# Key turns and scores one w_in slot sooner, the first two value products in the last two slots, and the first heads' products ahead of the wait for the chunk state's copy

## The chip, the cores and the metric

One core of a Trainium2 chip runs the whole step in one launch. The metric is the device time of one execution in microseconds, as the median of several runs. The engines are TensorE (PE; its weight loads are shown apart as PEld), VectorE (DVE), ScalarE (ACT), GpSimd (POOL) and SyncE (SP, which only issues DMAs here). Each engine works off its own list of instructions in order, and waits on semaphores that the others count up.

## What is computed

Two layers of a hybrid decoder, for a prompt of 256 tokens and 8 sampled sequences of 8 tokens, which makes T = 320 columns everywhere. Each layer is a half FFN, a mixer and another half FFN. The mixer, cut from the reference:

```python
z = h @ p['w_in']
gq, gk, gv, gg, glr, sq, sk, sv, cu = jnp.split(z, offs, axis=-1)
# gated linear attention over gq, gk, gv, in chunks with a carried state
o_gla, s_new = gla_chunked(q, k, v, log_a, s0)
# stick-breaking attention over paged keys and values of 2048 past tokens
#   z = q.k/sqrt(d) + bias;  w = exp(log_sigmoid(z) + sum of log(1-beta) over later keys)
o_sb = stick_breaking(q_sb, k_all, v_all, p['sb_bias'], q_pos, k_pos)
# causal depthwise conv (31 taps) over cu, LayerNorm, swish
mix = jnp.concatenate([o_gla, o_sb, y], axis=-1)
return mix @ p['w_out'], k_new, v_new, s_new, buf_new
```

The part that this change touches is the stick-breaking attention of the 64 sampled tokens over their cached keys, from the last pages to the first, since each weight needs the sum over all later keys.

## The kernel before

**Units.** A weight matrix goes through in tiles of 128 output columns, called units. Each is loaded by SP into one of eight slots of `raw`, split by ACT (`hi`, line 1119) and DVE (`lo`, line 1470) into a rounded part and a rest, and multiplied by PE with three matmuls for each of eight k tiles (lines 571 to 573), 24 in all. `w_in` has 23 units. The loops over m = 4 to 22 on PE, ACT and DVE are each one program step for one unit; "slot m" below is that step. Each engine has its own loop over m, and the order in it is written out by hand.

**What rides along in the slots.** The cached keys come in 16 half page groups h = 0 to 15, for four batches each. For h there is, in this order: PE turns the keys (`turn_keys`, line 772, eight transposes for two batches, twice), ACT copies them from the bank to `kT` (`copy_keys`, line 1274), PE makes the scores (`scores`, line 787), and for each pair of h, it = 0 to 7, ACT takes the scores out of bank 4 (`place_scores`, lines 1283 and 1284) and makes the softplus (`softplus`, lines 1289 and 1291), DVE sums it up backwards (`log_weights`, lines 1678, 1681 and 1683), ACT takes the exponential (`weights`, line 1296), PE turns the weights (`turn_weights`, line 864), ACT copies them (`place_weights`, line 1301) and PE multiplies them with the pages of values (`values`, line 882). `TURNS` says which h is turned in which slot; `scores(h - 1)` is made at the start of the slot that turns h, ahead of the unit. In slots with two h (10 and 12 before) the second turn and a second score product stand between k tiles of the unit. SP and POOL load the keys of h when h - 2 has been turned (`SLOT_OF`), and the pages of `values(it)` when the room is free.

**What each slot has besides.** `turn_state` at the end of slot 6 and ACT's `place_state` behind it; ACT's `place_queries` in slot 7, which writes the queries to `qb` (line 1237), from which `scores` reads, and which stands behind the first `copy_keys` of the slot; two sigmoids in slot 8; the decays and levels of the gated linear attention in slots 12 to 20 (`decays`, lines 1253 and 1255; `level_prompt` and `level_sample` on PE; `place_prompt`, `place_sample`, `scale` and `decay` on DVE); copies of the conv state in slot 12 (lines 1354 and 1355); the conv taps (line 1619), shared out over the slots by two tables, where taps count by four instructions; and `scaled_in` (lines 1667 and 1672), DVE's read of a unit's bank.

**Behind slot 22.** PE makes the scores of the prompt (`pz_products`, lines 992 and 993), all but the first of which wait for DVE's `scaled_in(22)`. Then come the state products (line 1008), `values(1)`, the wait for ACT's copy of the first state (`s1`, line 1382), `gla_outputs` for heads 0 and 1 (line 943), the wait for DVE's second state (`s2`, line 1805), `turn_weights(3)` (line 864) and so on. Key 0 is turned before the mixer in both layers, key 1 in layer 1 alone (`KEYS_EARLY`).

Of the kernel before, what the change touches and what calls it, by code (L numbers as in the profile page):

```python
# [153 lines left out]
def zin_done(at, m):  # L154

    if m < 13:
        return at("zin_dve", m + 1)
    return at("zin_act", m - 12) if m < 19 else at("zin_dve", m - 5)


def slots():

    slot = []
    for l in range(L):
# [11 lines left out]
BEFORE = [max((v for v in range(u) if SLOT[v] == SLOT[u]), default=None) for u in range(len(SLOT))]  # L176
TAPS_EARLY = {13: 1, 14: 1, 15: 1, 16: 1, 17: 1, 18: 1, 19: 1}
TAPS_LATE = {9: 2, 10: 2, 11: 2, 12: 1, 14: 2, 16: 2, 18: 2, 19: 1, 20: 3, 21: 2, 22: 2}
TURNS = {7: (0,), 8: (1,), 9: (2,), 10: (3, 4), 11: (5,), 12: (6, 7), 13: (8,), 14: (9,), 15: (10,), 16: (11,), 17: (12,), 18: (13,),
         19: (14,), 20: (15,), 21: (16,), 22: (17,)}  # L180
KEYS_EARLY = ((0,), (0, 1))
SLOT_OF = {h: m for m, hs in TURNS.items() for h in hs}
WEIGHTS_AT = {10: 0, 11: 1, 13: 2, 14: 3, 16: 4, 18: 5, 20: 6, 22: 7}
MEAN_BANK = (3, 5, 0, 1)


# [24 lines left out]
def build(nc, ins, outs):  # L211
# [106 lines left out]
    def in_bank(m):  # L318

        return bank[m if m < 7 else (m + 1) % 2]  # L320
# [28 lines left out]
    with nc.Block() as block:  # L349
# [198 lines left out]
        def _(pe):  # L548
# [66 lines left out]
            def x_mean(M, b_):  # L615
                pe.wait_ge(sm["sx_done"], M + 1)
                pe.matmul(b_[:, 0:T], cst_("mean_d"), sx[:, :], start=True, stop=True).then_inc(sm["x_mean"], 1)
# [54 lines left out]
            def keys_early_copied(l2, h):  # L672
                pe.wait_ge(sm["kt_copied"], 64 * l2 + 4 * h + 4)

            for l in range(L):
# [4 lines left out]
                def at(name, n):  # L680
                    return sm[name], l * per[name] + n
# [193 lines left out]
                def values(it):  # L875

                    pe.wait_ge(*at("wt_placed", it + 1))
                    pe.wait_ge(*at(f"vs_loaded{it % 2}", 128 * (it // 2 + 1)))
                    pe.wait_ge(*at(f"vp_loaded{it % 2}", 128 * (it // 2 + 1)))
                    for j in range(4):  # L880
                        for b in range(G):
                            last = pe.matmul(bank[7][32 * b:32 * b + 32, 0:256], wT[:, it, j, 32 * b:32 * b + 32],  # L882
                                             vpg[l][it % 2][:, b, j, :], start=False, stop=(j == 3 and it % 4 == 3), skip_group_check=True)
                    last.then_inc(sm["v_used"], 1)

                entry(U + U_IN, M1, [in_bank(m) for m in range(4)])
                for m in range(4, NIN):
                    u, out = U + U_IN + m, in_bank(m)[:, 0:T]
                    if m < 7:
                        if m == 4:  # L890
                            keys_early_copied(l, l)
                        unit(u, out, hh, hl)
                        if m == 4:
                            x_mean(M1, bank[7])
                        if m == 6:
                            turn_state()
                        continue
                    h, last_h = TURNS[m][0], TURNS[m][-1]
                    if h < 2 * ITS:
                        turn_keys(h, (0, 1))  # L900
                    if 0 < h <= 2 * ITS:
                        scores(h - 1)
                    if m == 8:
                        new_scores()
                    if 14 <= m < 18:
                        level_sample(m - 14)
                    if m == 22:
                        turn_khat()
                    pe.wait_ge(*zin_done(at, m - 7 if m < 9 else m - 2))
                    if h == last_h:  # L910
                        unit(u, out, hh, hl, part=range(4))
                    else:
                        unit(u, out, hh, hl, part=range(3))
                        turn_keys(h, (2, 3))
                        unit(u, out, hh, hl, part=range(3, 5))
                        turn_keys(last_h, (0, 1))
                        unit(u, out, hh, hl, part=range(5, 6))
                        scores(h)
                        unit(u, out, hh, hl, part=range(6, 7))
                    if last_h < 2 * ITS:  # L920
                        turn_keys(last_h, (2, 3))
                    if m == 9:
                        log_gates()
                    if m == 11:
                        turn_rows()
                        new_weights()
                    if m == 12:
                        turn_conv()
                    if 13 <= m < 21:
                        level_prompt(m - 13)  # L930
                    if 14 <= m < 20:
                        turn_values(m - 14)
                    if m == 22:
                        new_values(0)
                        values(0)
                    if m >= 20:
                        turn_weights(m - 20)
                    unit(u, out, hh, hl, part=range(4, KD) if h == last_h else range(7, KD))

                def gla_outputs(pair):  # L940

                    def mm(h, cols, lhs, rhs, first=False, end=False):
                        return pe.matmul(bank[O_BANK[h % 2]][:, cols], lhs, rhs, start=first, stop=end, skip_group_check=True)  # L943
                    vh = [slice(h * DV, (h + 1) * DV) for h in range(H)]
                    for h in pair:
                        mm(h, slice(0, P), gv[:, 0, vh[h]], att[:, 0, h, :], True)
                        mm(h, slice(P, TP), gv[:, 1, vh[h]], att[:, 1, h, :])
                        mm(h, slice(TP, T), gv[:, 2, vh[h]], att[:, 2, h, 0:TS])
                    for h in pair:
                        r, p_ = head(h)  # L950
                        mm(h, slice(P, TP), s1[r, p_, :], qt[r, 0, p_, P:TP])
                    for b in range(DB):
                        c = slice(TP + DT * b, TP + DT * b + DT)
                        for h in pair:
                            r, p_ = head(h)
                            last = mm(h, c, st[r, b, p_, :], qt[r, 0, p_, c], end=(b == DB - 1))
                            if b == DB - 1:
                                last.then_inc(sm["o_prod"], 1)
# [50 lines left out]
                                         kn[:, ch, h * DK:(h + 1) * DK], gv[:, ch, h * DV:(h + 1) * DV], start=True, stop=True, skip_group_check=True)  # L1009
                last.then_inc(sm["s1_prod"], 1)  # L1010

                values(1)
                pe.wait_ge(*at("s1_ready", 1))
                gla_outputs((0, 1))
                pe.wait_ge(*at("s2_ready", 2))
                turn_weights(3)
# [89 lines left out]
        def _(act):  # L1106
# [97 lines left out]
            for l in range(L):  # L1204
# [88 lines left out]
                def weights(it):  # L1293

                    act.wait_ge(*at("lw_ready", it + 1))
                    A(nsa(z_[:, it, :], z_[:, it, :], ACT.Exp), sm["w_ready"])
# [8 lines left out]
                for m in range(7, NIN):  # L1305
                    what = UNITS_IN[m][0]
                    for h in TURNS[m]:
                        if h < 2 * ITS:
# [3 lines left out]
                        if h >= 2 and h % 2 == 0:  # L1312
                            place_scores(h // 2 - 1)
                        if h == TURNS[m][0]:
                            hi(U + U_IN + m + 2)
# [12 lines left out]
                            A(nsa(tn[:, :, :], tn[:, :, :], ACT.Ln, bias=1.0), sm["zn_l"])  # L1328
                        if h >= 2 and h % 2 == 0:
                            softplus(h // 2 - 1)  # L1330
                    if m in WEIGHTS_AT and m < 22:
                        weights(WEIGHTS_AT[m])
                    if m == 9:
                        act.wait_ge(*at("loga_pre", 1))
# [33 lines left out]
                        place_values(m - 14)  # L1368
                    if m >= 20:
                        place_weights(m - 20)  # L1370
                    if m == 22:
                        weights(7)
                    if what in ("gv", "sv"):
                        act.wait_ge(sm["w_used"], U + U_IN + m + 1)
                        A(nsa(fT[:, 4 + (m + 1) % 2, :], in_bank(m)[:, 0:T], ACT.Copy), sm["zin_act"])
# [85 lines left out]
        def _(dve):  # L1461
# [133 lines left out]
            for l in range(L):  # L1595
# [4 lines left out]
                def at(name, n):  # L1600
                    return sm[name], l * per[name] + n
# [72 lines left out]
                def log_weights(it):  # L1674

                    z, s = z_[:, it, :], s_[it % 2]
                    dve.wait_ge(*at("z_l", it + 1))
                    V(dve.scalar_tensor_tensor(t_[:, :], z, 0.0, t_[:, :], ALU.max, ALU.add))
                    V.settle()
                    later = sn[:, it // 4, 0:1] if it % 4 == 0 else s_[1 - it % 2][:, 0:1]  # L1680
                    V(dve.tensor_tensor_scan(s[:, ::-1], cst_("ones", cols=1).to_broadcast([P, 512]), t_[:, ::-1], later, ALU.mult, ALU.add))
                    V.settle()
                    V(dve.tensor_tensor(z, z, s[:, :], ALU.subtract), sm["lw_ready"])
# [9 lines left out]
                for m in range(7, NIN):  # L1693
# [60 lines left out]
                    if 13 <= m < 19:  # L1754
                        if m > 13:
                            dve.wait_ge(*at("att_done", level_copies(m - 14)))
                        place_prompt(m - 13)
                    for h in TURNS[m]:
                        if h >= 2 and h % 2 == 0:
                            log_weights(h // 2 - 1)  # L1760
                    for k in range(TAPS_LATE.get(m, 0)):
                        conv(taps)
                        taps += 1
# [117 lines left out]
def head(h):  # L1881

    return slice((h % 2) * DK, (h % 2 + 1) * DK), h // 2
# [35 lines left out]
```

## Time and profile before

| | us |
|---|---|
| median of 3 runs | 1443.51 |
| lowest, highest | 1441.48, 1445.41 |
| the profiled execution | 1444.73 |
| its span | 1443.1 |
| PE busy | 1405.8 (97%) |
| DVE busy | 899.5 (62%) |
| ACT busy | 738.4 (51%) |

The profiled execution lies 1.2 us above the median. Its span is 1.6 us shorter than its device time. The mixer's slots of layer 0 lie between 274 and 406 us of the span, those of layer 1 706 us later. In the rows, L is a line of the kernel, and a tile is named as out<-in with its buffer number left out.

### The profile page before, as it was taken

The numbers are of one execution on the slowest core, as the hardware profiler recorded it, in microseconds if no ns is written. First come the engines' busy times: TensorE is split into PE (matmuls) and PEld (weight loads), VectorE is DVE, ScalarE is ACT, GpSimd is POOL, SyncE is SP. The second block draws the span as 40 slices with busy tenths as digits, with TensorE's granted clock in tenths as the row PEclk, the third lists the DMA queues.
The fourth block names the chain that finished last, engine by engine and source line by source line (L and its number), as shares of the span: only waits on it lengthen the run. The fifth ranks groups of instructions, "written<-read, shape, count | busy, mean of one in ns | idle before, by whom it ended". The sixth has DMA issues, their size and how long they took to land.

```text
span 1443.1 us, 26817 instructions
## 1 busy us (share of the span) xinstructions
PE 1405.8 (97%) x10515; PEld 1329.7 (92%) x10515; DVE 899.5 (62%) x1496; ACT 738.4 (51%) x1198; POOL 179.6 (12%) x326
## 2 busy tenths in 40 slices
PE   7999999999999999999999999999999999999997
PEld 6999999988877899999999999999887689999996
DVE  5665633679985766653367655355899747766542
ACT  4544433588855544343364444355886555443431
POOL 0020000323254000000000000021423510000000
PEclk9999999999999999999999999999999999999998
DMA  9565555567798575545545555556867894554441
GB/s 239 147 204 150 145 150 156 163 199 223 212 294 270 149 189 153 146 139 156 156 130 151 146 146 146 146 153 176 249 201 232 270 250 130 150 154 146 147 135 37
DMA packets 391362, 250.23 MB, mean 173 GB/s; under 512 B 14369, under 2 KB 379446, under 8 KB 391236
## 3 DMA queue, kind: packets, MB, share of 16 engines
q1 hardware_dynamic: 375602, 205.86, 50.0%
q0 software_dynamic: 15328, 42.52, 9.5%
q8 instruction: 84, 1.38, 0.4%
q14 instruction: 42, 0.34, 0.1%
q10 hardware_dynamic: 306, 0.13, 0.0%
HBM read 242.91 MB, written 5.53 MB: 172 GB/s over the span
## 4 chain that ended last, share of the span: by engine, by line
PE 89%; DVE 5%; ACT 3%; DMA 2%; issue 1%; SPq 0%; ACTq 0%
PE bank L571 23%; PE bank L572 23%; PE bank L573 23%; PE bank L772 3%; PE bank L882 2%; PE bank L607 2%; PE bank L611 2%; PE bank L608 2%; DVE fT L1619 2%; PE bank L787 2%; PE bank L943 1%; PE bank L737 1%; DVE w_l L1470 1%; DMA raw<-in_ffn_w_up 1%; DMA raw<-in_ffn_w_gate 1%
## 5 line engine op out<-in xcount | busy, mean ns | idle before, releaser
L1470 DVE TENSOR_TENSOR w_l<-raw,w_h 128x1024 fp32r<-128x1024 f32 (+1 forms) x334 | 397.6, 1197 | 301.7 <-ACT w_h L1119 301.7
L571 PE MATMUL bank<-hh,w_h 128*128 128x320 f32 x1648 | 517.5, 314 | 0.0
L573 PE MATMUL bank<-hh,w_l 128*128 128x320 f32 x1648 | 509.2, 309 | 0.0
L572 PE MATMUL bank<-hl,w_h 128*128 128x320 f32 x1648 | 509.1, 309 | 0.0
L1119 ACT ACTIVATE w_h<-raw 128x1024 fp32r<-128x1024 f32 (+1 forms) x334 | 334.6, 1030 | 144.2 <-DMA raw<-in_ffn_w_down 98.8
L571 PEld LDWEIGHTS bank<-hh,w_h 128*128 128x128 f32 x1648 | 309.4, 188 | 11.4 <-issue 8.6
L572 PEld LDWEIGHTS bank<-hl,w_h 128*128 128x128 f32 x1648 | 309.6, 188 | 0.5
L573 PEld LDWEIGHTS bank<-hh,w_l 128*128 128x128 f32 x1648 | 309.4, 188 | 0.0
L573 PE MATMUL bank<-guh,w_l 128*128 128x320 f32 x704 | 217.4, 309 | 0.0
L571 PE MATMUL bank<-guh,w_h 128*128 128x320 f32 x704 | 217.4, 309 | 0.0
L572 PE MATMUL bank<-gul,w_h 128*128 128x320 f32 x704 | 217.4, 309 | 0.0
L571 PEld LDWEIGHTS bank<-guh,w_h 128*128 128x128 f32 x704 | 132.2, 188 | 0.0
L572 PEld LDWEIGHTS bank<-gul,w_h 128*128 128x128 f32 x704 | 132.2, 188 | 0.0
L573 PEld LDWEIGHTS bank<-guh,w_l 128*128 128x128 f32 x704 | 132.2, 188 | 0.0
L1188 ACT ACTIVATE sg<-gr 128x320 f32<-128x320 f32 x88 | 41.5, 472 | 170.5 <-DVE gr L1537 170.4
L1193 ACT ACTIVATE guh<-gt 128x320 fp32r<-128x320 f32 x88 | 41.5, 472 | 131.0 <-DVE gt L1548 131.0
L499 POOL DMA_DIRECT2D st<-in_state_gla x4 | 3.6, 900 | 652.6 <-PE bank L573 652.6
L471 POOL DMA_DIRECT2D kpg<-in_cache_sb_k x112 | 60.6, 541 | 163.2 <-PE bank L772 135.6
L1537 DVE TENSOR_TENSOR gr<-bank,rs 128x320 f32<-128x320 f32 x88 | 43.0, 488 | 60.4 <-PE bank L573 45.3
L1619 DVE SCALAR_TENSOR_TENSOR fT<-ext,par_all,fT 128x256 f32<-128x256 f32 x240 | 76.4, 380 | 2.1
L1274 ACT ACTIVATE kT<-bank 128x512 f32<-128x512 f32 x116 | 62.8, 595 | 22.1 <-PE bank L772 21.7
L772 PE MATMUL bank<-const,kpg 128*128 128x128 f32 x448 | 58.5, 273 | 0.7 <-ACT kT L1274 0.7
(268 smaller groups left out, 1601.7 us busy)
## 6 DMA issues: line engine op xcount, KB each, us to landing
raw<-in_ffn_w_gate SPq DMA_DIRECT2D x88, 512.0 KB, 3.9
raw<-in_ffn_w_up SPq DMA_DIRECT2D x88, 512.0 KB, 3.9
raw<-in_ffn_w_down SPq DMA_DIRECT2D x64, 448.0 KB, 3.7
raw<-in_w_in SPq DMA_DIRECT2D x46, 512.0 KB, 4.1
raw<-in_ffn_w_down SPq DMA_DIRECT2D x32, 512.0 KB, 4.0
kpg<-in_cache_sb_k SPq DMA_DIRECT2D x112, 128.0 KB, 3.1
kpg<-in_cache_sb_k POOLq DMA_DIRECT2D x112, 128.0 KB, 2.6
raw<-in_w_out SPq DMA_DIRECT2D x16, 512.0 KB, 8.1
```

The costliest lines, as they stand in the source:

```text
L471: pool.dma_start(heads(kpg[l][:, h % 2, b, j, :]), page(pool, ids[4 * i + 2 * (h % 2) + j], ins["cache_sb_k"], l)).then_inc(sm[f"kp_loaded ...
L571: pe.matmul(out, w_h[:, slot, k, :], rhs_h[:, k0 + k, :], start=first, stop=False)
L572: pe.matmul(out, w_h[:, slot, k, :], rhs_l[:, k0 + k, :], start=False, stop=False)
L573: last = pe.matmul(out, w_l[:, slot, k, :], rhs_h[:, k0 + k, :], start=False, stop=end)
L772: last = pe.transpose(bank[2 + b % 2][:, p_ * 256 + j * P:p_ * 256 + (j + 1) * P], src[:, b, j, p_ * P:(p_ + 1) * P], cst_("ident"))
L1119: A(nsa(w_h[:, slot, 0:n, :], raw[:, slot, 0:n, :], ACT.Copy), sm["w_hi"])
L1188: A(nsa(sg[:, t, :], gr[:, t, :], ACT.Silu), sm["gate_act"])
L1193: A(nsa(guh[:, 2 * i + t, :], gt[:, t, :], ACT.Copy), sm["gu_hi"])
L1274: A(nsa(kT[l][:, h % 2, b].rearrange("p a c -> p (a c)"), bank[2 + b % 2][:, :], ACT.Copy), sm["kt_copied"])
L1470: V(dve.tensor_tensor(w_l[:, slot, 0:n, :], raw[:, slot, 0:n, :], w_h[:, slot, 0:n, :].bitcast(F32), ALU.subtract), sm["w_lo"])
L1537: V(dve.tensor_tensor(gr[:, t, :], ffn_bank(i, 2 * t)[:, 0:T], rs[:, :], ALU.mult), sm["gate_r"])
L1619: V(dve.scalar_tensor_tensor(out, x, par("conv_w", 2 * k + c), out, ALU.mult, ALU.add), sm["conv_y"] if k == TAPS - 1 and c == n == 1 else ...
```

## The change

The key turns 1 to 15 and the scores 0 to 15 are each made one slot sooner: h = 1 in slot 7, and two of them in slots 10 (4 and 5) and 12 (7 and 8). `weights(it)` moves one slot sooner from it = 2 on. DVE's `log_weights` has a table of its own: it = 0 and 1 stay in slots 9 and 10, the others move one slot sooner. `new_values(0)` and `values(0)` move from slot 22 to slot 21, and `values(1)` from behind the state products into slot 22. The wait for `s1_ready` moves into `gla_outputs`, behind the first six products of the two heads.

```diff
-TURNS = {7: (0,), 8: (1,), 9: (2,), 10: (3, 4), 11: (5,), 12: (6, 7), 13: (8,), 14: (9,), 15: (10,), 16: (11,), 17: (12,), 18: (13,),
-         19: (14,), 20: (15,), 21: (16,), 22: (17,)}
+TURNS = {7: (1,), 8: (2,), 9: (3,), 10: (4, 5), 11: (6,), 12: (7, 8), 13: (9,), 14: (10,), 15: (11,), 16: (12,), 17: (13,), 18: (14,),
+         19: (15,), 20: (16,), 21: (17,), 22: (17,)}
...
-WEIGHTS_AT = {10: 0, 11: 1, 13: 2, 14: 3, 16: 4, 18: 5, 20: 6, 22: 7}
+WEIGHTS_AT = {10: 0, 11: 1, 12: 2, 13: 3, 15: 4, 17: 5, 19: 6, 21: 7}
+LOGS_AT = {9: 0, 10: 1, 11: 2, 12: 3, 14: 4, 16: 5, 18: 6, 20: 7}
...
-                    if m == 22:
+                    if m == 21:
                         new_values(0)
-                        values(0)
+                    if m >= 21:
+                        values(m - 21)
...
                         mm(h, slice(TP, T), gv[:, 2, vh[h]], att[:, 2, h, 0:TS])
+                    pe.wait_ge(*at("s1_ready", 1))
                     for h in pair:
...
-                values(1)
-                pe.wait_ge(*at("s1_ready", 1))
                 gla_outputs((0, 1))
...
-                    if m in WEIGHTS_AT and m < 22:
+                    if m in WEIGHTS_AT:
                         weights(WEIGHTS_AT[m])
...
-                    if m == 22:
-                        weights(7)
...
-                    for h in TURNS[m]:
-                        if h >= 2 and h % 2 == 0:
-                            log_weights(h // 2 - 1)
+                    if m in LOGS_AT:
+                        log_weights(LOGS_AT[m])
```

## Rows read from the trace of the kernel before

**Rows 1.** The page, busy time of each engine over the whole span.
```profile
PE 1405.8 (97%) x10515; PEld 1329.7 (92%) x10515; DVE 899.5 (62%) x1496; ACT 738.4 (51%) x1198; POOL 179.6 (12%) x326
```

**Rows 2.** Waits of PE: who waited for whom: us in total, times, longest.
```profile
PE bank L607 <- ACT hh L1146: 8.9, 5, 2.8
...
PE bank L992 <- DVE fT L1672: 2.7, 2, 1.7
...
PE bank L882 <- DMA vpg1a<-in_cache_sb_v: 0.9, 1, 0.9
PE bank L772 <- ACT kT L1274: 0.7, 2, 0.3
PE bank L752 <- DVE att L1651: 0.6, 2, 0.3
```

**Rows 3.** Windows, DVE: stretch, length, busy (instructions), PE's granted clock, DMA.
```profile
345.10:361.90 16.80, 16.52 (x38) 1.00 0.65 189
378.32:408.52 30.20, 28.52 (x65) 1.00 0.75 226
```

**Rows 4.** Timeline, PE, slots 7 and 8, layer 0: start, length, instruction, tiles.
```profile
282.32 0.39 PE L571 MATMUL bank<-hh,w_h 128*128 128x320 f32 x1
...
285.93 1.04 PE L772 MATMUL bank<-const,kpz 128*128 128x128 f32 x8
```

**Rows 5.** Timeline, ACT, slot 7, layer 0.
```profile
284.27 0.82 ACT L1237 ACTIVATE qb<-qs 64x64 f32<-64x64 f32 x4
```

**Rows 6.** Timeline, ACT, slots 12 and 13, layer 0.
```profile
327.04 1.09 ACT L1274 ACTIVATE kT<-bank 128x512 f32<-128x512 f32 x2 [1.12 <-PE bank L772]
328.01 0.74 ACT L1253 ACTIVATE dd<-dd 128x640 f32<-128x640 f32 x1
...
331.57 1.07 ACT L1274 ACTIVATE kT<-bank 128x512 f32<-128x512 f32 x2
332.52 0.69 ACT L1283 ACTIVATE z__105<-bank,bq 128x512 f32<-128x512 f32 x1
...
336.95 0.62 ACT L1296 ACTIVATE z__105<-z__105 128x512 f32<-128x512 f32 x1
```

**Rows 7.** Timelines, PE and ACT, slot 7, layer 1.
```profile
990.04 0.39 PE L571 MATMUL bank<-hh,w_h 128*128 128x320 f32 x1
...
991.98 0.82 ACT L1237 ACTIVATE qb<-qs 64x64 f32<-64x64 f32 x4
```

**Rows 8.** Timeline, PE, slots 12 and 13, layer 0.
```profile
325.86 0.41 PE L571 MATMUL bank<-hh,w_h 128*128 128x320 f32 x1
...
332.29 1.11 PE L772 MATMUL bank<-const,kpg 128*128 128x128 f32 x8
```

**Rows 9.** Timeline, DVE, the scan of a log, slot 15, layer 0.
```profile
355.68 1.29 DVE L1681 TENSOR_TENSOR_SCAN s<-const,sn,t__106 128x512 f32<-128x512 f32 x1
```

**Rows 10.** Timelines, behind slot 22: PE in layers 0 and 1, DVE in 1.
```profile
411.98 2.62 PE L882 MATMUL bank<-vpg0b,wT 128*32 128x256 f32 x32
...
1117.06 1.93 PE L882 MATMUL bank<-vpg1b,wT 128*32 128x256 f32 x32
...
1122.52 0.66 PE L864 MATMUL bank<-const,z__105 128*128 128x128 f32 x4
...
1119.67 0.60 DVE L1805 SCALAR_TENSOR_TENSOR s<-s,aend,bank 128x128 f32<-128x128 f32 x2
```

**Rows 11.** Windows with the clock: all engines; PE alone at both FFN entries.
```profile
410.02:413.43 3.41, 3.41 (x33) 2.35 (x36) 3.19 (x10) 1.31 (x3) 0.00 (x0) 0.50 0.92 291
...
485.11:491.94 6.83, 5.94 (x22) 5.94 (x23) 6.80 (x16) 4.87 (x11) 0.00 (x0) 0.50 0.17 44
...
486.00:502.85 16.85, 16.85 (x97) 0.82 0.02 5
1193.03:1207.35 14.32, 14.32 (x96) 1.00 0.00 1
```

**Rows 12.** Waits of all engines: DVE's logs for ACT's softplus.
```profile
DVE t__106 L1678 <- ACT t__106 L1291: 12.0, 4, 4.8
```

## The prediction

> **What bounds the kernel now.** I read the page's busy times first, then PE's waits, then the timelines of the three compute engines side by side through the mixer of layer 0, from 282 to 415 us, and of layer 1 the same places. PE is busy for 97% of the span [rows 1], so an edit pays only where it removes a wait of PE, and costs wherever it adds one. PE's waits inside the mixer are few [rows 2]: 2.7 us in both layers together for DVE's last `scaled_in` ahead of `pz_products`, 0.9 us for a load of value pages in layer 1, 0.7 us for ACT's key copies (slot 11) and 0.6 us for DVE's `place_prompt` (slot 14). The matmuls, transposes and scores that move are the same in number, so their time is only moved. All that the change can win is therefore about 5 us, and half of it is one wait.
>
> The wait at `pz_products` has a cause of its own. From the end of slot 18 to the last `scaled_in`, DVE is busy for 28.52 of 30.20 us, and in slots 15 and 16 for 16.52 of 16.80 [rows 3]. DVE is a second engine at its limit there, and the change takes no work from it.
>
> **Slot 7, the first key turn and scores.** Before, slot 7 had nothing but the unit's 24 matmuls between `turn_state` and `scores(0)`; these ran from 282.32 to 285.93 us [rows 4]. They covered what ACT must do meanwhile: place the state, split weight tile 8 and only then copy the queries into `qb`, from 284.27 for 0.82 us [rows 5]. After the change `scores(0)` stands ahead of the unit, and it waits for `qb_ready`. In layer 0, PE starts turn 1 at 282.32; eight transposes take 1.0 us (1.04 with the end of the last) [rows 4], so it would be at the scores at 283.3. ACT now has turn 1's first two key copies in front of the queries, since `copy_keys` is called before `place_queries`: 284.27, plus 1.0 for two copies (1.09 with its end) [rows 6], plus 0.82, is 286.1. **PE waits 2.9 us** with the hand-over. In layer 1 key 1 was turned early, so there are no transposes and no copies: PE is there at 990.04 and the queries are ready at 991.98 + 0.82 = 992.8 [rows 7]. **PE waits 2.8 us.** Behind PE's wait stand the unit of slot 7 and everything after it, and no engine has work ahead that could give the time back, because ACT and DVE are fed by PE's units. Sum: +5.7 us. Bounds: 5.5 to 5.9; I find nothing that hides it.
>
> **Slots 8 to 11.** ACT does the first `place_scores` and `softplus` one slot sooner, in the slot with the two sigmoids. Following its queue against PE's, the copies are ready when PE asks for them, in slot 9 with about 0.1 us to spare. In slot 11 ACT no longer has slot 10's `softplus` just ahead of the copies that PE waits for, so the 0.34 us of that wait goes in each layer: -0.7.
>
> **Slots 12 and 13.** Here the change loads ACT. `scores(7)` is now the second score product of slot 12, so `place_scores(3)` and `softplus(3)` stand in slot 12 behind it, with `weights(2)`, all ahead of `decays(1)`, the two copies for the conv state and `decays(2)`, and all of it ahead of the copy of turn 9 that PE needs for the second half of that turn. In the times of the kernel before: the matmuls behind the slot's second score product start at 325.86 [rows 8]; `place_scores` takes 1.2 (two of 0.69), two copies 1.0, `weights` 0.6 (0.62), `softplus` 1.3 (two activations on a tile of the same size as that of `weights`), decays and conv copies 331.57 - 328.01 = 3.56, the first copy of the next turn 0.54, half of 1.09 [rows 6]. That ends at 334.1. PE was at this turn at 332.29 [rows 8]: **1.8 us of waiting**, and 0.3 more where turn 8 in slot 12 finds ACT late from slot 11. Together 2.1 in each layer, +4.2. Bounds: 0 if ACT's queue is shorter than I add it up, 2.6 if nothing overlaps.
>
> **Slots 14 to 19.** The logs now fall into the even slots, where two late conv taps are; odd slots have neither. Two slots take 16.8 us, of which DVE works 16.5 [rows 3], some 8.3 in each; a log is a scan of 1.3 us [rows 9] and two passes of about half of it, 2.7 together. So DVE needs 8.3 + 2.7 = 11.0 us from the start of `place_sample` in an even slot to that in the next. PE asks for the next one after a slot of 8.4 and the stretch from `level_sample` to `level_prompt`, four k tiles of the unit and half a key turn, 2.8: 11.2. With `place_sample` itself (0.5) DVE is late by up to 0.4. Two such places, +0.8 a layer. Slot 14's own wait for `place_prompt` (0.3) goes, as there are no logs in slot 13. Net +0.5 a layer, +1.0. Bounds: -0.6 (only the gain) to +2.
>
> **Slots 18 to 22.** Slots 20 and 21 lose a turn and a score product (3 us), and `values(0)` and `values(1)` (1.93 us each) stand in 21 and 22. PE reaches `pz_products` no later than now, but DVE still has the same 28.5 us behind slot 18. What it can save is its own idle time there, 1.7 us at most [rows 3], hand-overs included. I take 0.7 a layer, about in the middle: -1.4, bounds -2.7 (the whole of the wait) and 0. The value pages are asked for a slot sooner and used a slot sooner; the load's 0.9 us [rows 2] is gone, or falls under the wait for DVE, so it is worth nothing by itself.
>
> **Behind slot 22.** `values(1)` stood between the state products and `gla_outputs`, 1.93 us in layer 1 [rows 10], and hid ACT's copy of `s1`; now the six products of the first heads stand there, so no wait appears. PE is at the turn behind the wait for `s2_ready` at 1122.5 in layer 1; without `values(1)` it is there at 1120.6, and `s2` is written at 1119.67 + 0.60 = 1120.3 [rows 10]. Cost 0, with 0.3 us to spare; up to 0.5 a layer if DVE slips.
>
> **The clock.** New waits of some 3 us matter twice. PE sat idle for 2.8 us at the entry of the second FFN in both layers (its wait for ACT's `hh` [rows 2] is the row of it). In layer 0 the granted clock then was 0.50 (1.2 GHz) for 6.83 us, in layer 1 it stayed at 1.00 (2.4 GHz) behind an idle time of the same length; the same entry matmuls took 16.85 us in the first and 14.32 in the second [rows 11]. A fall so costs 2.5 us. The Trainium skill (TensorE: Matmul & The Clock Gate, the section on HAM oscillation in real kernels) puts the loss at half of the time at half clock; that is an estimate of 3.4 us for these 6.83, and by it my sum would be 0.9 higher. The measured 2.5 stands. The wait of 1.7 us at `pz_products` in layer 0 was also followed by 3.4 us at 0.50: `values(1)` took 2.62 us instead of 1.93 [rows 10, 11]. Of four new waits of 2 to 3 us I count one fall of 2.5 (bounds 0 and three, 7.5), and leave the one at `pz_products` as it is.
>
> **Sum.** 5.7 - 0.7 + 4.2 + 1.0 - 1.4 + 2.5 = +11.3 us. The profiled execution took 1444.73 us (span 1443.1), which gives 1456.0; it stood 1.2 above the median of 1443.51, so I predict **1454.8 us**.
>
> **The rivals.**
> *Only slot 7 waits.* ACT catches up in slot 12 because its steps overlap more than I add; then 4.2 and most of the clock term go: 1443.5 + 5.7 - 0.7 + 1.0 - 1.4 = 1448 without a fall, 1450.6 with one. For it: ACT is busy only 51% of the span [rows 1]. Against: the steps of [rows 6] follow one another without a gap already. Chance 0.20, a third of it within 0.3%.
> *The tail pays it back.* Slot 7 costs its 5.7, but the pz wait (2.7), the load (0.9) and the key copies (0.7) all go, and `values(1)` runs at full clock (0.7): 1443.5 + 0.7 = 1444. It needs DVE to be through 1.3 us sooner in each layer than now. Chance 0.07.
> *Faster: DVE sets the time of the mixer, not PE.* If the chain of slots 14 to 22 on DVE is the bound from end to end, earlier scores let it start its logs sooner (it sat idle for 4.8 us before one of them [rows 12]), the wait in slot 7 is absorbed, and PE's waits of 2.7, 0.9, 0.7 and 0.6 go with the slow `values(1)` (0.7): 1443.5 - 5.6 = 1438. It decides if PE loses less than 1.3 us in slot 7. Chance 0.06.
> *More falls of the clock:* two more, 1454.8 + 5 = 1460. Chance 0.08.
> The forecast itself has 0.59.
>
> **How the numbers follow.** This kernel's measurement can tell 0.3% from no change, 4.3 us: below 1439.2 is faster, above 1447.8 slower. Slower: 0.59 + 0.08 + two thirds of 0.20 = 0.80. Same: 0.07 + 0.07 = 0.14. Faster: 0.06. The range goes from 1447 (only slot 7, most of the pz wait gone) to 1462 (both ACT waits in full, two or three falls) and leaves out the last two cases of the other sign and a little above.
>
> **What would show it.** Right: in the profile after, PE's line of the scores waits for ACT's `qb` copy, 2 times, 5 to 6 us in all; its line of the turns waits for the `kT` copies for 3 to 5 us in slot 13; the pz wait still stands at 1.5 us or more in sum; the window of DVE behind slot 18 holds 28.5 us of work as before. Wrong: a wait for `qb` under 1 us would break the largest step; no wait in slot 13 the second; a pz wait of zero would say that DVE had more to give than its idle time.

## The result, and the profile after

| | before | after |
|---|---|---|
| median, us | 1443.87 (6 runs, 1441.48 to 1445.41) | 1455.56 (6 runs, 1452.45 to 1458.58) |
| ratio | | 1.0087, 95% interval 1.0074 to 1.0100 |
| profiled execution, us | 1444.73 | 1458.58 |
| its span | 1443.1 | 1456.9 |
| PE busy in it | 1405.8 | 1410.4 |
| span less PE busy | 37.3 | 46.5 |

The changed kernel is 11.7 us slower; the forecast was 11.3 (1454.8 us), inside its range. The profiled execution lies 3.0 above the median, so its span is 13.8 longer than that of before. Two of the runs in the next section, one of g2 (1973.1 us) and one of h1 (1540.7 us), were at mean granted clocks of 0.65 and 0.85 and are left out of the medians and ratios.

The first thing to read is the busy line of the page, beside [rows 1]:

```profile
PE 1410.4 (97%) x10515; PEld 1334.7 (92%) x10515; DVE 900.1 (62%) x1496; ACT 739.2 (51%) x1198; POOL 179.2 (12%) x326
```

No engine has another number of instructions, and DVE and ACT are busy for as long as before (within 0.8 us). PE is busy for 4.6 us more with the same 10515 matmuls, and idle for 9.2 us more (46.5 - 37.3). The 13.8 us are the sum of these two. The idle time is in the waits of PE (us in total, times, longest), to be read against [rows 2]; line numbers on PE and ACT are one higher than before, those on DVE one lower:

```profile
PE bank L608 <- ACT hh L1147: 8.9, 5, 2.8
...
PE bank L788 <- ACT qb L1238: 5.4, 2, 2.8
PE bank L883 <- ACT wT L1302: 4.1, 6, 0.7
PE bank L773 <- ACT kT L1275: 3.7, 2, 1.9
PE bank L967 <- ACT wT L1302: 1.4, 1, 1.4
PE bank L995 <- DVE fT L1671: 1.3, 2, 0.7
PE bank L738 <- DVE att L1657: 1.2, 4, 0.3
...
PE bank L883 <- DMA vpg1a<-in_cache_sb_v: 0.8, 1, 0.8
PE bank L851 <- DVE qt L1748: 0.7, 1, 0.7
```

L788 is new, and so are L967, L738 and L851; L773 had 0.7 us in slot 11 and now has 3.7 in slot 13; the wait at `pz_products` (L995) has halved; the one for `place_prompt` is gone. That for the page `vpg1a` is still there (0.8 us, 0.9 before). The timelines of ACT and PE in slot 7 of layer 0 (start, length, instruction, tiles, wait in brackets) show the largest one, where [rows 4, 5] showed none:

```profile
284.34 1.09 ACT L1275 ACTIVATE kT<-bank 128x512 f32<-128x512 f32 x2
285.29 0.83 ACT L1238 ACTIVATE qb<-qs 64x64 f32<-64x64 f32 x4
...
286.27 1.17 PE L788 MATMUL bank<-kpz,qb 128*32 128x256 f32 x16 [2.76 <-ACT qb L1238]
```

PE is through with its transposes at 283.5 and stands still until the second copy of keys and then the four copies of queries are done. In slot 13, ACT's queue ahead of the copy that PE wants is this, against [rows 6, 8]:

```profile
333.81 1.09 ACT L1275 ACTIVATE kT<-bank 128x512 f32<-128x512 f32 x2
334.93 0.63 ACT L1290 ACTIVATE t__106<-t__106 128x512 f32<-128x512 f32 x1
335.59 0.63 ACT L1292 ACTIVATE t__106<-t__106 128x512 f32<-128x512 f32 x1
336.13 0.62 ACT L1297 ACTIVATE z__105<-z__105 128x512 f32<-128x512 f32 x1
336.65 0.72 ACT L1254 ACTIVATE dd<-dd 128x640 f32<-128x640 f32 x1
...
340.18 1.07 ACT L1275 ACTIVATE kT<-bank 128x512 f32<-128x512 f32 x2
...
340.90 1.29 PE L773 MATMUL bank<-const,kpg 128*128 128x128 f32 x8 [1.87 <-ACT kT L1275]
```

The 4.6 us of PE's busy time are its clock. The windows behind the four long waits (length, then PE, PEld, DVE, ACT and POOL busy, then the granted clock) show 0.50 each time, that is 1.2 GHz; before, no such stretch stood in the slots:

```profile
287.10:290.50 3.40, 3.40 (x19) 3.13 (x13) 1.23 (x1) 0.11 (x1) 0.00 (x0) 0.50 0.02 5
341.70:345.10 3.40, 3.40 (x23) 2.85 (x21) 3.37 (x7) 3.35 (x6) 2.18 (x4) 0.50 0.44 122
1000.50:1003.90 3.40, 3.40 (x19) 2.95 (x12) 1.23 (x1) 1.94 (x3) 0.00 (x0) 0.50 0.00 0
1055.10:1058.50 3.40, 3.40 (x21) 3.18 (x18) 3.37 (x8) 2.57 (x5) 1.93 (x4) 0.50 0.52 154
```

Behind slot 22 is a wait that the prediction did not have, at the head means (L967):

```profile
423.84 0.63 ACT L1403 ACTIVATE ps_t<-ps_t 128x512 f32<-128x512 f32 x1
425.46 0.63 ACT L1401 ACTIVATE ps_t<-ps_t 128x512 f32<-128x512 f32 x1 [0.98 <-DVE ps_t L1799]
426.12 0.63 ACT L1403 ACTIVATE ps_t<-ps_t 128x512 f32<-128x512 f32 x1
426.65 0.75 ACT L1386 ACTIVATE osq<-bank 128x320 f32<-128x320 f32 x2
427.29 0.60 ACT L1302 ACTIVATE wT<-bank 128x512 f32<-128x512 f32 x1
...
424.62 1.94 PE L883 MATMUL bank<-vpg0a,wT 128*32 128x256 f32 x32
427.99 0.78 PE L967 MATMUL bank<-osq,const 128*128 128x320 f32 x2 [1.43 <-ACT wT L1302]
```

ACT's squares and its `place_weights(3)` stand behind the softplus of the third prompt score (L1401, L1403), which waits for DVE. While `values(1)` stood between the state products and `gla_outputs`, PE came here 1.93 us later and this queue was hidden. g1 and g2 below bear this out: with the values' half left out the wait is absent, with the values' half alone it stands in both layers (2.9 us in two).

### The profile page after: what moved, and what is told of

The parts are those of the page before. It is cut to its first block, busy times and chain, and to the rows that moved or that the text cites. A ratio compares the mean times of both kernels' runs of the same rounds, so it can differ in the third digit from the quotient of the medians.

```text
span 1456.9 us, 26817 instructions
## 1 busy us (share of the span) xinstructions
PE 1410.4 (97%) x10515; PEld 1334.7 (92%) x10515; DVE 900.1 (62%) x1496; ACT 739.2 (51%) x1198; POOL 179.2 (12%) x326
## 4 chain that ended last, share of the span: by engine, by line
PE 86%; DVE 9%; ACT 3%; issue 1%; DMA 1%; SPq 0%; ACTq 0%
PE bank L572 23%; PE bank L573 22%; PE bank L574 22%; DVE fT L1618 3%; PE bank L773 2%; PE bank L608 2%; PE bank L612 2%; PE bank L609 2%; PE bank L788 2%; PE bank L883 2%; DVE w_l L1469 1%; PE bank L945 1%; DVE s L1680 1%; DMA raw<-in_ffn_w_gate 1%; PE bank L985 1%
## 5 line engine op out<-in xcount | busy, mean ns | idle before, releaser
L773 PE MATMUL bank<-const,kpg 128*128 128x128 f32 x448 | 58.5, 273 | 3.7 <-ACT kT L1275 3.7
```

Of the source, the lines that this page charges most:

```text
L773: last = pe.transpose(bank[2 + b % 2][:, p_ * 256 + j * P:p_ * 256 + (j + 1) * P], src[:, b, j, p_ * P:(p_ + 1) * P], cst_("ident"))
```

## The experiments

The table gives for each kernel the median, the ratio to the kernel before measured beside it (whose medians were 1442.3 to 1443.9; differences to it below are to the one beside), and three readings of its profiled execution: PE busy, the span less that, and the time at a granted clock of 0.50 (without the last 13 to 15 us of the program, which are at 0.50 in all of them).

| | median | ratio, 95% interval | span | PE busy | rest | at 0.50 |
|---|---|---|---|---|---|---|
| before | 1443.5 | | 1443.1 | 1405.8 | 37.3 | 17.1 |
| after | 1455.56 | 1.0087, 1.0074 to 1.0100 | 1456.9 | 1410.4 | 46.5 | 27.3 |
| e1_queries_first | 1446.12 | 1.0023, 1.0011 to 1.0035 | 1443.8 | 1401.2 | 42.6 | 6.8 |
| e2_softplus_later | 1458.53 | 1.0105, 1.0076 to 1.0133 | 1455.7 | 1406.9 | 48.8 | 20.5 |
| e3_both | 1448.63 | 1.0035, 1.0022 to 1.0047 | 1446.1 | 1405.1 | 41.0 | 17.1 |
| e4_wait_alone | 1451.18 | 1.0064, 1.0041 to 1.0087 | 1446.9 | 1402.6 | 44.3 | 10.2 |
| f1_taps_odd | 1445.98 | 1.0017, 1.0003 to 1.0030 | 1444.3 | 1406.1 | 38.2 | 17.1 |
| f2_taps_tail | 1445.33 | 1.0010, 0.9997 to 1.0023 | 1438.7 | 1400.6 | 38.1 | 6.8 |
| f3_all | 1438.94 | 0.9975, 0.9960 to 0.9990 | 1437.1 | 1402.1 | 35.0 | 10.2 |
| f4_before_taps | 1450.96 | 1.0047, 1.0016 to 1.0078 | 1447.5 | 1406.2 | 41.3 | 20.5 |
| g1_keys_alone | 1470.92 | 1.0176, 1.0142 to 1.0210 | 1471.2 | 1417.0 | 54.2 | 44.4 |
| g2_values_alone | 1453.32 | 1.0067, 1.0043 to 1.0091 | 1450.0 | 1404.0 | 46.0 | 17.1 |
| g3_all_values_late | 1449.39 | 1.0056, 1.0034 to 1.0079 | 1445.5 | 1404.8 | 40.7 | 17.1 |
| h1_queries_tail | 1444.58 | 1.0015, 1.0004 to 1.0025 | 1442.0 | 1403.7 | 38.3 | 13.7 |

All of them execute the same 10515 matmuls, so the columns can be read against each other. PE's busy time goes with the time at half clock: from f2 (6.8 at 0.50) to g1 (44.4) it grows by 16.4, which is 0.44 us for each us at half clock; the straight line through all rows of the table has 0.43, and no row is further than 1.3 us from it. In some of these stretches PE waits for a part of the time. Against the part in which it was busy (6.8 us in f2, 41.8 in g1) the line has 0.47, and no row is further than 0.7 us from it. So the time of a profile can be split into what the kernel waits and what its clock costs.

### e1_queries_first: ACT copies the queries ahead of the state

The changed kernel, with ACT's `place_queries` at the end of slot 6, ahead of `place_state`.

```diff
+                place_queries()
                 place_state()
                 hi(U + U_IN + 8)
...
-                        if m == 7:
-                            place_queries()
```

> The changed kernel with one thing undone: ACT copies the queries into qb before it places the state, so they are ready when PE comes to scores(0) in slot 7. Theory (the wait in slot 7 is paid in full, since nothing runs ahead of PE): PE's wait for qb (5.4 us in two) goes, with the two stretches at half clock behind it (1.3 us each), so 1455.6 - 5.4 - 2.6 = about 1448, ratio to before 1.003; the 1.9 us waits in slot 13 stay. Rival (DVE, which has the logs and two late taps in the even slots, sets the time): PE only comes to DVE's waits sooner, the waits for att, qt and fT grow by what is saved, and the time stays within 1 us of 1455.

Measured: 1446.12, 9.4 us less than after; about 1448 had been expected. ACT now writes the queries when it would otherwise sit idle, and PE's scores follow its transposes at once:

```profile
275.77 0.83 ACT L1238 ACTIVATE qb<-qs 64x64 f32<-64x64 f32 x4 [1.28 <-DVE qs L1665]
...
281.59 1.04 PE L773 MATMUL bank<-const,kpz 128*128 128x128 f32 x8
282.56 1.07 PE L788 MATMUL bank<-kpz,qb 128*32 128x256 f32 x16
```

The wait of 5.4 us is gone and 20.5 us fewer are at half clock, 9.2 less in PE's busy time; the head means' wait now shows in both layers (2.9 instead of 1.4). In the profiled executions that makes -3.9 - 9.2 = -13.1; that of after was 3 us above its median. The step at slot 7 is the largest part of the loss, as forecast.

### e4_wait_alone: the same wait in the kernel before

Nothing is moved; PE must have seen the queries' copy before the unit of slot 7.

```diff
+                    if m == 7:
+                        pe.wait_ge(*at("qb_ready", 4))
                     pe.wait_ge(*zin_done(at, m - 7 if m < 9 else m - 2))
```

> The kernel before with nothing moved, but PE made to wait in slot 7, ahead of the unit, for the queries that scores(0) needs a slot later: the wait without the change. Theory: PE idles 2.8 us in each layer, nothing gives it back, and if the clock falls behind it 1.3 us more each: 1443.9 + 5.6 + 0 to 2.6 = 1449.5 to 1452. Rival (a late PE in slot 7 lets DVE catch up, which is late at slot 22): the wait of 2.7 us at the prompt scores shrinks by as much as PE is late, so only 3 of 5.6 us stay: 1447 or less.

```profile
PE bank L571 <- ACT qb L1239: 5.2, 2, 2.6
...
PE bank L994 <- DVE fT L1674: 2.5, 2, 1.4
PE bank L882 <- DMA vpg0b<-in_cache_sb_v: 2.3, 1, 2.3
PE bank L882 <- DMA vpg1b<-in_cache_sb_v: 1.1, 1, 1.1
```

Measured: 1451.18, +8.2. The rival "DVE sets the time of the mixer and absorbs slot 7" falls here: with PE 2.6 us later in each layer, its wait for DVE at the prompt scores only went from 2.7 to 2.5 us. DVE too is fed by PE's units and came 2.6 us later itself: its last `scaled_in` of layer 0 starts at 410.59 us, at 408.03 in the kernel before. The wait is paid in full, and waits for value pages come on top; why these appear was not tested.

### e2_softplus_later: the load of slot 12 on ACT moved on

The changed kernel, with `softplus(3)`, `weights(2)` and `log_weights(3)` in slot 13 and `weights(3)` in 14.

```diff
-WEIGHTS_AT = {10: 0, 11: 1, 12: 2, 13: 3, 15: 4, 17: 5, 19: 6, 21: 7}
-LOGS_AT = {9: 0, 10: 1, 11: 2, 12: 3, 14: 4, 16: 5, 18: 6, 20: 7}
+WEIGHTS_AT = {10: 0, 11: 1, 13: 2, 14: 3, 15: 4, 17: 5, 19: 6, 21: 7}
+LOGS_AT = {9: 0, 10: 1, 11: 2, 13: 3, 14: 4, 16: 5, 18: 6, 20: 7}
...
-                        if h >= 2 and h % 2 == 0:
+                        if h >= 2 and h % 2 == 0 and h != 8 or h == 9:
```

> The changed kernel with softplus(3) and weights(2) put off from slot 12 to slot 13 (and the log behind them, weights(3) from 13 to 14), so that ACT has 1.9 us less ahead of the key copy that PE needs in slot 13. Theory (ACT's queue in slot 12 is what is late): the two waits of 1.87 us for kT in slot 13 go, and two stretches at half clock with them: 1455.6 - 3.7 - 2.6 = about 1449; the wait for qb stays at 5.4. Rival (PE gets the copy sooner, but then waits for DVE, whose log now stands in slot 13): a new wait for att or qt of about 1.5 us in each layer, time 1454.

Measured: 1458.53, not below after (the intervals of the two ratios overlap). The wait for `kT` in slot 13 is gone, so ACT's queue in slot 12 was its cause. In its place PE waits for DVE, 2.0 us in slot 15 of each layer, as the rival had it:

```profile
PE bank L738 <- DVE att L1657: 4.6, 4, 2.0
```

DVE's timeline ahead of it, from the first log at 343.92 us on, has two logs and two late taps (eight instructions) with one gap of 0.4 us. So DVE has no room for another log between slots 13 and 15; the term "slots 14 to 19" of the prediction has its reason here. The new wait cancels the old one, and the head means' wait now shows in both layers; that the median came out 3 us above after goes with a lower mean granted clock (0.9865, after 0.9893) and is not explained further.

### e3_both: e1 and e2 together

> Both edits on the changed kernel at once. Theory (the two waits are separate and add up): 1455.6 - 9.1 - 4 to 5 of half clock = about 1442, ratio 0.998 to 1.000; what is left of the change against before is a shorter wait at the prompt scores (1.3 instead of 2.7 us) against new waits for DVE in slots 15 and 17 and at the khat turn (1.2 and 0.7) and for ACT at the head means (1.4). Rival (the earlier scores themselves cost something else, such as key loads that come too late): over 1446, with a wait of PE for kpg or kT.

Measured: 1448.63, 2.5 more than e1. The sum of the two gains did not come. The rival's number (over 1446) did, but not for its reason: PE waits neither for a key page nor for `kT`. e2's edit is worth nothing while the taps stand where they are: it removes 3.7 us of waits for ACT, adds 3.4 at L738, and the clock of e3 was the worse (17.1 us at 0.50 against 6.8).

### f1, f2, f3: give the engines room, one step at a time

f1 is e1 with the two taps of slots 14, 16 and 18 in the odd slots, where no log is.

```diff
-TAPS_LATE = {9: 2, 10: 2, 11: 2, 12: 1, 14: 2, 16: 2, 18: 2, 19: 1, 20: 3, 21: 2, 22: 2}
+TAPS_LATE = {9: 2, 10: 2, 11: 2, 12: 1, 13: 2, 15: 2, 17: 2, 19: 1, 20: 3, 21: 2, 22: 2}
```

> The kernel with the queries first (1446.1), and the two late conv taps of slots 14, 16 and 18 put into 13, 15 and 17, where DVE has no log. Theory (logs and taps in the same slots make DVE late): PE's waits for att in slots 15 and 17 (1.2 us), for qt (0.7) and for the last bank read (1.2) go for the most part, 1446.1 - 3 = 1443; the waits for kT in slot 13 (3.7) and at the head means (2.9) stay. Rival (DVE's work is simply too much, wherever it stands): the waits for DVE move but keep their sum of 3.1 us, time 1446.

f2 is f1 with ACT's squares and `place_weights(3)` behind the second softplus of the prompt scores.

```diff
                     A(nsa(ps_t[:, n, :], ps_t[:, n, :], ACT.Ln, bias=1.0), sm["pz_l"])
-                squares((0, 1))
-                place_weights(3)
+                    if n == 1:
+                        squares((0, 1))
+                        place_weights(3)
```

> As the one before, and ACT reads the first two heads and copies the turned weights 3 ahead of the third softplus of the prompt instead of behind it. Theory (values(1) used to hide ACT's wait for DVE there, and its removal laid it open): the waits of 1.43 us at the head means go in both layers, 3 us less than the kernel with the taps moved alone, about 1440. Rival (DVE's third pass, not ACT's order, is what PE waits for): PE then waits as long at the next step, the running sums of the prompt, and the time is the same within 0.5 us.

f3 is f2 with e2's edit and the two taps of slot 13 in slot 12.

> As the one before, and softplus(3), weights(2) and the log behind them put off from slot 12 to 13, with the taps of slot 13 in slot 12. Theory (the first try of this failed because DVE had two logs and two taps in a row; now it has not): the waits of 1.87 us for kT in slot 13 go without a new one for att in slot 15 (2.0 us before), 3.7 us less than the kernel before it, about 1436.5. Rival (two logs in slots 13 and 14 alone are too much for DVE): a wait for att in slot 15 of 1 us or more in each layer, and 1438 to 1440.

Measured: f1 1445.98, f2 1445.33, f3 1438.94. In f1 the waits at L738 (1.2 us) are gone and the gain is not there (-0.1 against e1; 1443 had been expected). Its profile has 4.4 us less of waits than e1's and 4.9 us more of busy PE: 17.1 us at half clock instead of 6.8. The mean granted clock of all its runs says the same, 0.9907 against 0.9932, which is 0.0025 * 1445 * 2 = 7 us more at half clock, 3 us of time. The wait at the head means is missing in f1's profile only because `values(2)` in front of it ran at half clock (3.20 us in layer 0, 1.93 in e1). f2 differs from f1 by less than these runs can tell. Its profiled execution was the fastest of its runs, 5.0 us below their median, so its row of the table shows it at its best. f3 takes away the last wait above 0.7 us in the slots, and it is faster than both kernels, 3.3 us below the one before:

```profile
PE bank L883 <- ACT wT L1302: 4.1, 6, 0.7
...
PE bank L995 <- DVE fT L1671: 1.2, 2, 0.6
PE bank L851 <- DVE qt L1748: 0.7, 2, 0.5
PE bank L883 <- DMA vpg1a<-in_cache_sb_v: 0.6, 1, 0.6
```

Neither `qb`, `kT`, `att` nor the head means is left among its waits of PE. The time is in the rival's range (1438 to 1440), but the wait for `att` that the rival named is not there. The change as such can so be made to pay a little, when ACT's and DVE's steps are moved along with PE's.

### h1_queries_tail: the missed wait behind slot 22 alone

e1 with f2's edit on ACT.

> e1_queries_first with one order changed behind slot 22: ACT makes the squares and the copy of the weights of values(3) behind the second softplus of the prompt scores, not behind the third. Theory (that order is what opened the wait of PE at the head means, 1.4 us in each layer, when values(1) no longer stood in front): the wait goes, and the time is that of e1_queries_first less 2.9, 1443.2. Rival (a wait removed there is given back by the clock or by the next wait, as in f1_taps_odd): 1445 to 1447.

Measured: 1444.58, between the two numbers expected; the wait at L967 (2.9 us in e1) is gone. Of the 2.9 us 1.5 came out by the medians, 1.2 by the ratios. The mean granted clock of the runs went from 0.9932 to 0.9911, by the same sum 2.7 us of time, more than what is missing. So the cause of the wait is shown, and that its 2.9 us cannot be booked in full; that the lower clock follows from the removed wait is only argued.

### g1, g2: the two halves of the change alone

g1 is the changed kernel with the value products and the wait for `s1` as before; g2 is the kernel before with only these moved.

```diff
-                    if m == 21:
-                        new_values(0)
-                    if m >= 21:
-                        values(m - 21)
+                    if m == 22:
+                        new_values(0)
+                        values(0)
...
-                    pe.wait_ge(*at("s1_ready", 1))
                     for h in pair:
...
+                values(1)
+                pe.wait_ge(*at("s1_ready", 1))
                 gla_outputs((0, 1))
```

(The diff is g1's; g2's is its reverse, in the kernel before.)

> Only the first half of the change: turns, scores, weights and logs one slot sooner; the value products and the wait for s1 stand as before the change. Theory (the slots cost it, and the tail of the change gives a little back): the waits of the changed kernel in slots 7 (5.4 us), 13 (3.7) and 15/17 (1.2) all stay; PE reaches the prompt scores 1.93 us sooner in each layer, as values(1) is not in slot 22, while DVE is no sooner, so that wait grows from 0.7 to 2 to 2.6 us each; the head means no longer wait for ACT (-1.4). Time 1455 to 1459. Rival (the tail of the change costs as much as the slots): waits as in the changed kernel, and 1449 to 1452.

> Only the second half of the change: keys as before the change, values(0) in slot 21, values(1) in slot 22, the wait for s1 behind the first heads' products. Theory (the pages set it: POOL may ask for them only when key 15 has been turned): GpSimd issues the pages of values(0) from 1097.2 to 1102.5 us in layer 1 of the kernel before and they land some 4 us later, at 1106; PE is at the product at 1099 when it stands a slot sooner, so it waits 6 to 7 us in each layer for vpg0a and vpg1a. Against that go the waits at the prompt scores (2.7) and for the page in slot 22 (0.9). With two or three falls of the clock 1453 to 1461. Rival (the second half is free by itself, or wins the wait at the prompt scores): 1440 to 1444.

Measured: g1 1470.92, 27 us above the kernel before and far off both numbers expected; g2 1453.32, +9.6, inside its theory's 1453 to 1461. g1's waits:

```profile
PE bank L851 <- DVE qt L1748: 6.8, 2, 3.4
...
PE bank L788 <- ACT qb L1238: 5.4, 2, 2.8
...
PE bank L773 <- ACT kT L1275: 3.7, 2, 1.9
PE bank L883 <- DMA vpg1b<-in_cache_sb_v: 3.6, 1, 3.6
```

Slots 20 and 21 have lost a turn and a score product, so PE comes to `turn_khat` in slot 22 3.4 us before DVE has written `qt`: 6.8 us for nothing. With `new_values(0)` and `values(0)` in slot 21 PE spends 2.6 us of the 3.4 (403.87 to 406.47 us in layer 0 of after) on work that it has to do in any case, and 0.7 stay as its wait for `qt`. In layer 1 the 0.8 us for `vpg1a` stand in their place. The rest of g1's excess over after is a page load and 17 us more at half clock (6.6 us in PE busy). In g2 the pages are what is missing, for 4.9 and 5.4 us where 6 to 7 had been expected:

```profile
PE bank L882 <- DMA vpg1a<-in_cache_sb_v: 5.4, 1, 5.4
PE bank L882 <- DMA vpg0a<-in_cache_sb_v: 4.9, 1, 4.9
```

and in the timelines of POOL and PE in layer 1:

```profile
1099.10 0.54 POOL L484 DMA_DIRECT2D vpg1a<-in_cache_sb_v  x1 [13.45 <-PE bank L772]
1100.24 4.17 POOL L484 DMA_DIRECT2D vpg1a<-in_cache_sb_v  x7 [0.61 <-issue]
...
1110.17 2.36 PE L882 MATMUL bank<-vpg1a,wT 128*32 128x256 f32 x20 [5.40 <-DMA vpg1a<-in_cache_sb_v]
```

POOL may ask for them only when key 15 has been turned (its wait is for PE's L772). Besides, g2 has the wait at the head means in both layers (2.9 us), which g1 does not have: it belongs to the values' half. So each half alone costs, and the two do not add up to the whole: +27.2 and +9.6 alone, +11.7 together. The keys' half gives PE idle time at the end and lets the pages be asked for sooner; the values' half is what uses both.

### g3, f4: room for DVE without the values' half

g3 is f3 with the values as before. f4 is the kernel before with one tap of slot 20 and one of slot 22 made in slots 10 and 11.

```diff
-TAPS_LATE = {9: 2, 10: 2, 11: 2, 12: 1, 14: 2, 16: 2, 18: 2, 19: 1, 20: 3, 21: 2, 22: 2}
+TAPS_LATE = {9: 2, 10: 3, 11: 3, 12: 1, 14: 2, 16: 2, 18: 2, 19: 1, 20: 2, 21: 2, 22: 1}
```

> f3_all with the second half of the change taken back (values(0) in slot 22, values(1) behind the state products, the wait for s1 in front of all six products). Theory (moving the values is what lets PE use the time that DVE wins, and what brings the later pages in time): PE waits 2 us or more for DVE at the prompt scores in each layer, or 2 to 4 us in sum for vpg0b and vpg1b; time 1442 to 1447. Rival (the gain of f3_all comes from the slots alone and the place of the values does nothing): 1438 to 1440.

> The kernel before with nothing moved but two conv taps: from slots 20 and 22 to 10 and 11, where DVE waits for ACT. Theory (the wait at the prompt scores comes from DVE's load in slots 18 to 22): DVE is 2.5 us sooner there and the waits of 1.7 and 1.0 us go, with the half clock behind the first: 1443.5 - 2.7 - 0.7 = about 1440.5. Rival (DVE in slots 10 to 12 has no room either): PE's wait for att in slot 14 grows from 0.3 us by as much, and the time is the same.

Measured: g3 1449.39, 10.5 above f3 and above both numbers expected; f4 1450.96, 8.7 above the kernel before, where a gain had been expected. In g3 it is L851 again (6.7 us, 3.4 a layer), not the prompt scores, where 0.2 us is left. In f4 the wait at the prompt scores did go (2.7 us), and this came for it:

```profile
PE bank L882 <- ACT wT L1301: 5.5, 7, 1.3
PE bank L882 <- DMA vpg1b<-in_cache_sb_v: 3.4, 1, 3.4
...
PE bank L737 <- DVE gk L1672: 1.6, 2, 0.8
```

POOL asked for the pages of `values(2)`, `values(3)` and `values(4)` of layer 1 from 1113.8, 1121.4 and 1127.4, so 7.6 and 6.0 us apart, where it had been 8.7 and 7.5; the longest load into `vpg1b` took 8.4 us from issue to landing (6.4 before). That the closer requests made it longer is argued from these numbers, not tested. The median of f4 has a range from 1442.3 to 1455.2, which stays open. What its profile shows is that a wait of PE for DVE can be worth nothing: in layer 1 the wait of 1.0 us went, and one of 3.4 us for a page stood behind it.

## Why the prediction was right, step by step

**Slot 7, +5.7 predicted.** Measured 2.76 + 2.67 = 5.4, by e1 (removed) and e4 (alone). Right, to 0.3 us.

**Slots 8 to 11, -0.7.** The wait of slot 11 is gone. Right.

**Slots 12 and 13, +4.2.** The wait in slot 13 is 1.87 us in each layer where 1.8 was predicted; the 0.3 in slot 12 does not exist. 3.7 in all; e2 shows that ACT's queue is its cause. Adding up the queue's lengths from the rows of before worked, since its steps follow one another without a gap. The 0.3 that was added for slot 12 had no row behind it.

**Slots 14 to 19, +1.0.** 0.3 us at each of four places (L738, 1.2), less the 0.6 at `place_prompt`: +0.6. Right in place and sign, 0.3 where 0.4 was taken.

**Slots 18 to 22, -1.4.** The wait at the prompt scores went from 2.7 to 1.3: -1.4. The value was taken from the middle of its bounds, so that it came out is luck, and the prediction's own sign for it (1.5 us or more left) was missed by 0.2. The load's wait, taken as gone or hidden, still stands (0.8 us), which costs the sum nothing. And the step takes the two halves of the change as one. It names what they do together and not that without the values' half the loss would be 6.8 us one step earlier, at `turn_khat`, where 0.7 us is left now (L851), which was not forecast either.

**Behind slot 22, 0.** This step failed. It looked at `s1` and `s2`, which were in time as forecast, and left the rest of ACT's queue out: the squares and `place_weights(3)` behind a softplus that waits for DVE. Cost 1.4 us in layer 0. In layer 1 the wait does not show, as `values(2)` ran at half clock and took 3.35 us instead of 1.93, which is the same 1.4 us in another form; e1 has both waits.

```profile
1137.52 3.35 PE L883 MATMUL bank<-vpg1a,wT 128*32 128x256 f32 x32
```

**The clock, +2.5.** The mechanism was right and its size was not: too few falls, and too long ones. I counted one fall of 6.83 us among four waits. The clock fell behind all four, for 3.4 us each. Against them, two stretches of before are gone: the one behind the wait at `pz_products` in layer 0 (410.02 us), which I had meant to leave as it is, and one at 1123.4 us. One of 3.4 us is new, at the entry of the second FFN in layer 1 (1205.3 us). Three are left over: 27.3 - 17.1 = 10.2 us at half clock, 4.6 us of busy PE, 1.5 a fall. The price of 2.5 us was itself read too low per us. It is 0.37 for each of the 6.83 us of [rows 11], but PE was busy for only 5.94 of them, which makes 0.43 for a busy us; the fourteen profiles have 0.47. Half of the time at half clock, as the Trainium skill has it (TensorE: Matmul & The Clock Gate, the section on HAM oscillation), would give an estimate of 5.1. The trace's 4.6 lies a little below that. Over all runs the difference is smaller: mean granted clock 0.9907 before (in the runs beside e1 to e4) and 0.9893 after, 4 us at half clock, 1.8 us of time.

**The sum.** Waits: predicted 5.7 - 0.7 + 4.2 + 1.0 - 1.4 = 8.8, measured 9.2 (the terms named above, with 1.4 behind slot 22 and 0.7 at L851, add up to 9.7; small waits elsewhere make the rest). By the profiled executions 9.2 + 4.6 = 13.8; by the medians 9.2 + 1.8 = 11.0 of the 11.7 measured. That 11.3 was so near is in part luck: too little at the tail and in the number of falls stands against too much in what a kernel's runs lose to them on average.

**The rivals.** "Only slot 7 waits" fell with L773 in slot 13. "The tail pays it back" fell: L995 kept 1.3 us, and a new wait came behind it. "DVE absorbs slot 7" fell with e4. "More falls" is half true: in the profiled execution, not in the median.

## What to carry to other kernels

When steps of one engine are moved sooner, list for each the queue of the engine that feeds it, up to the place where it now stands, and add the lengths; here that gave the two long new waits to 0.3 us. Do the same for what a removed step had covered, with every instruction of the other engine's queue and not only the one that PE names in its wait. And test parts of a change together and alone: here a part that costs 27 us and one that costs 10 cost 12 together, and gain 3 when ACT's and DVE's orders follow.

## What the runs showed of the chip

A wait of PE in the middle of the work came with a fall of the granted clock from 1.00 to 0.50 far more often than I had taken. All eight waits of 2.6 to 2.8 us in slot 7 (after, e2, e4 and g1, both layers) had one, 9 of the 12 waits of 1.9 us in slot 13 (after, e1, f1, f2, g1, h1), and 3 of the 4 of 2.0 us in slot 15 (e2, e3). The falls began between 0.9 us ahead of the end of the wait and 1.6 us behind it, and lasted 3.4 us, once 6.8. The wait of 2.8 us at the entry of the second FFN, where the prediction had seen one fall in two, had one in 23 of its 28 cases in the fourteen profiles. None of the nine waits of 1.4 us at the head means (after, e1, e2, e3 and g2) had one. Not every fall has such a wait in front of it: f3 had 3.4 us at 0.50 from 427.7 and from 1117.2, behind no idle time over 0.7 us. What these have in common was not settled. f1 and f2 show how much hangs on it: their profiled executions wait equally long (38.2 and 38.1 us), were at 0.50 for 17.1 and 6.8 us, and their spans are 5.6 us apart. A wait of 1 us that is removed cannot be seen through that in a few runs.
